# A hybrid Hyena / RG-LRU / latent-attention kernel: the attention's output projection begun inside attention, two layer norms in halves, two steps of the mixer in another order

## The chip, the cores and the metric

The kernel runs on one core of a Trainium2 chip. The number that counts is the device time of one execution in microseconds (us); lower is better. The engines are PE (TensorE, matrix products), DVE (VectorE), ACT (ScalarE), POOL (GpSimd) and SP (SyncE, whose queue issues most DMAs). PEld is PE's loading of the stationary operand, shown apart from the products that stream through it.

## The reference

Two layers work on 512 latent tokens and 256 context tokens of width 1024. A layer is half a SwiGLU feed-forward net, a token mixer, and another half net; each sub-layer is modulated and ends in a layer norm:

```python
x_lat = half_ffn(x_lat, ...)                                  # ends in a layer norm
h_lat = modulate(x_lat, m_lat[3], m_lat[4])
y_lat, y_ctx = even_mixer(...) if l % 2 == 0 else odd_mixer(...)
x_lat = layernorm(ALPHA * x_lat + m_lat[5] * y_lat, ln_g[l, 1], ln_b[l, 1])
x_lat = half_ffn(x_lat, ...)                                  # last layer: latent tokens alone

def layernorm(x, g, b):
    mu = jnp.mean(x, -1); var = jnp.mean((x - mu) ** 2, -1)
    return (x - mu) * lax.rsqrt(var + LN_EPS) * g + b

# odd_mixer: 16 heads of latent attention, 512 queries, 768 keys
o_l = blocked_attention(qn_l, qr_l, k_nope, k_rope, v)        # softmax over keys
out_lat = o_l.reshape(B, L, MLA_HEADS * MLA_V) @ w_out        # 1024 x 1024

# even_mixer: y = x0 * (longconv(v * x1) + bias * ...), beside a gated linear recurrence
Y = rfft(u, n=2 * L) * rfft(k, n=2 * L); y = irfft(Y)[:L]
```

Everything is float32.

## The kernel before, in words

Activations lie in SBUF with the channels on the 128 partitions, in 8 chunks (m or k = 0 to 7), and the tokens along the free axis: 512 latent, then 256 context. A float32 product is made of three: the weight and the activation are each split into a high part (rounded to fp32r) and the rest, and PE adds high x high, high x low and low x high in PSUM (lines 2768 to 2770). Weights come by DMA in pieces of 512 KB (128 x 1024) into two buffers, RAW[0] and RAW[1], by turns. ACT makes the high part of a piece (WHI, line 990), DVE the low part (WLO, line 1619); a piece's buffer is loaded again when its low part is done. There are three pairs of such weight buffers: A, B and W, each for two pieces ("a unit").

All five engines run programs written out by hand, each with its own order, tied by semaphores. An engine that waits holds everything behind it in its program. So the place of an instruction in the code sets the order.

**Even mixer (layer 0).** `even_in` makes its input in ten units; in the last (u == 9) `turned_product` (line 3155) turns the convolution's input by 24 transposes in six groups of four, three PSUM banks in turn; group 3 waits until ACT has taken group 0 (`ut_ok`). Then six forward transforms (`forward(n)`, n = 0 to 5: two for the context, four for the latent tokens) each end in `spectrum(n)` on DVE (line 2397), which multiplies by the filter's spectrum; `recur(7)` (line 2357) is the last of eight steps of the recurrence, 5 instructions on DVE. SP loads the table of a transform (`slab_load`) and the filter's spectrum (`spectra_load`); for n = 4 and 5 both wait for `spectrum(n-2)`. Then come the inverse transforms (lines 3252 and 3261) and the output projection `ev_out`.

**Odd mixer (layer 1).** Attention runs in 64 steps g = 8 i + s: i is the pair of heads, s = 0 to 7 a head's block of 128 queries. In step g PE makes the scores of g (lines 2768 to 2770), turns the probabilities of g - 2 by six transposes (line 3381), and adds half of the values' product of an earlier step (line 3396). DVE takes the row's maximum (line 2620), the low part of the turned probabilities (PTL, line 2598), and scales the probabilities (PR, line 2628). ACT makes the exponential (line 1473) and the high part (PTH, line 1481). POOL makes low parts of queries and keys, and of the heads' outputs (OLO, line 900). A pair of heads gives one chunk of the projection's input, OHI[k] and OLO[k]; the first seven are there before step 63, the eighth only after attention's last product. The projection's eight chunks m, 24 products of 512 columns each, begin behind that (`odd_out`); their units use the weight buffers A, B, A, B. DVE adds each chunk to X (line 2470).

**Layer norm.** PE sums over partitions with a matrix of ones (line 2780), ACT takes the mean MU, DVE centers the 8 chunks (line 1736), ACT squares (line 1222), PE sums the squares (line 2792), ACT takes the root (line 1227), DVE the reciprocal (line 1742), and DVE multiplies the chunks (line 1749). For the next net ACT makes the modulated input H and its high part (lines 979 and 982), DVE its low part HLO (line 1719), and PE starts on chunk k when its HLO is there (lines 2817 to 2819). While both latent and context tokens are alive, these are two parts, one worked on while the other's products run. In the last layer the context is dropped behind the odd mixer, so `ln4` (behind attention) and `final` (at the end) have one part of 512 tokens.

**The end.** After `final`, DVE applies gain and bias (line 2654), PE turns X back (line 3452), ACT copies (line 1557), SP stores four tiles of 512 KB.

## Time and profile before

| | us |
|---|---|
| median of 3 runs | 3003.37 (2999.09 to 3003.84) |
| the profiled execution | 3004.83 |
| its span, first to last instruction | 3003.0 |
| PE busy, in the span | 2886.5 |

PE is the busy engine almost throughout. The page's end times of products are modelled and a product's shown duration overlaps the next, so the pace of PE is read from the starts of products, or from the regular distance of the DVE instructions that take their results. In the timeline a row is one instruction or several alike ("x6"), with the start, the length, and in brackets how long the engine had been idle and what ended that. The places that the change touches are about 885 to 945 us (the mixer's transforms), 2495 to 2625 us (attention's end to the first products of the last net, `ffn3`) and 2950 to 3003 us (the end).

### The profile page before, as it was taken

What the parts mean: (1) busy time and instruction counts of PE and PEld (TensorE: products, weight loads), DVE (VectorE), ACT (ScalarE), POOL (GpSimd) and SP (SyncE); (2) the same over time, 40 slices, a digit from 0 to 9 for tenths busy, and PEclk for the clock granted to TensorE, in tenths of its full rate; (3) what the DMA queues carried; (4) which work ended last, traced back from release to release, by engine and by line L of the source; (5) the groups of instructions that cost most, each with busy time, mean ns of one, the idle gap of its engine ahead of it and who ended that gap; (6) DMA issues with size and microseconds to landing.
All of it is one profiled execution on the core that took longest, in us unless ns stands there. A gap on an engine that the chain in (4) does not pass through costs nothing.

```text
span 3003.0 us, 43415 instructions
## 1 busy us (share of the span) xinstructions
PE 2886.5 (96%) x15883; PEld 2467.9 (82%) x15883; DVE 2035.9 (68%) x3216; ACT 1033.5 (34%) x1586; POOL 283.7 (9%) x393
## 2 busy tenths in 40 slices
PE   5999999999999999999999999999999998899997
PEld 2588989987884878898988899999878997688885
DVE  3377777777668477676776887777776886545444
ACT  0422233325650232232223433332255664422121
POOL 1001000001100100101001000000105561000000
PEclk7899999999999999999999999999999998999998
DMA  7334442221203233444431122222310101233330
GB/s 274 128 118 152 132 142 77 69 71 44 60 28 129 79 118 112 157 132 155 131 96 57 43 64 77 70 63 63 93 40 24 26 19 50 70 105 98 98 98 28
DMA packets 301116, 269.59 MB, mean 90 GB/s; under 512 B 31111, under 2 KB 257263, under 8 KB 300880
## 3 DMA queue, kind: packets, MB, share of 16 engines
q1 hardware_dynamic: 278384, 188.95, 21.0%
q0 software_dynamic: 21760, 76.03, 7.2%
q10 hardware_dynamic: 864, 3.15, 0.3%
q8 instruction: 70, 1.15, 0.2%
q14 instruction: 38, 0.31, 0.0%
HBM read 262.85 MB, written 5.24 MB: 89 GB/s over the span
## 4 chain that ended last, share of the span: by engine, by line
PE 89%; DVE 6%; ACT 2%; DMA 2%; issue 1%; POOL 1%; SPq 0%; ACTq 0%; DVEq 0%; POOLq 0%
PE PSALL L2768 15%; PE PSALL L2770 15%; PE PSALL L2769 15%; PE PSALL L3011 8%; PE PSALL L3012 8%; PE PSALL L3013 8%; PE PSALL L2817 2%; PE PSALL L2689 2%; PE PSALL L2818 2%; PE PSALL L2819 2%; PE PSALL L2792 2%; PE PSALL L3396 1%; PE PSALL L3381 1%; PE PSALL L2731 1%; PE PSALL L3261 1%
## 5 line engine op out<-in xcount | busy, mean ns | idle before, releaser
L1927 DVE SCALAR_TENSOR_TENSOR X<-PSALL,GATE,X 128x512 f32<-128x512 f32 x480 | 279.6, 612 | 102.0 <-PE PSALL L2770 101.4
L3011 PE MATMUL PSALL<-HHI,WSH 128*128 128x384 f32 x816 | 274.8, 337 | 5.6 <-DVE HLO L2125 5.6
L3012 PE MATMUL PSALL<-HLO,WSH 128*128 128x384 f32 x816 | 274.3, 336 | 0.0
L3013 PE MATMUL PSALL<-HHI,WSL 128*128 128x384 f32 x816 | 274.2, 336 | 0.0
L2768 PE MATMUL PSALL<-GHIA,WHIW 128*128 128x512 f32 (+1 forms) x616 | 217.5, 353 | 13.0 <-DVE X L1927 9.9
L2769 PE MATMUL PSALL<-GLOA,WHIW 128*128 128x512 f32 (+1 forms) x616 | 213.7, 347 | 0.0
L2770 PE MATMUL PSALL<-GHIA,WLOW 128*128 128x512 f32 (+1 forms) x616 | 213.1, 346 | 0.0
L2770 PE MATMUL PSALL<-GHIB,WLOW 128*128 128x512 f32 (+1 forms) x616 | 212.8, 346 | 0.0
L2768 PE MATMUL PSALL<-GHIB,WHIW 128*128 128x512 f32 (+1 forms) x616 | 212.8, 345 | 0.0
L2769 PE MATMUL PSALL<-GLOB,WHIW 128*128 128x512 f32 (+1 forms) x616 | 212.7, 345 | 0.0
L3011 PE MATMUL PSALL<-TH,WSH 128*128 128x384 f32 x612 | 208.6, 341 | 0.0
L3012 PE MATMUL PSALL<-TL,WSH 128*128 128x384 f32 x612 | 207.6, 339 | 0.0
L3013 PE MATMUL PSALL<-TH,WSL 128*128 128x384 f32 x612 | 207.5, 339 | 0.0
L1099 ACT ACTIVATE WSH<-RAW 128x512 fp32r<-128x512 f32 x204 | 129.1, 633 | 224.5 <-DVE RAW L2004 151.5
L2768 PE MATMUL PSALL<-HHI,WHIA 128*128 128x512 f32 (+1 forms) x464 | 168.7, 364 | 0.0
L2770 PE MATMUL PSALL<-HHI,WLOA 128*128 128x512 f32 (+1 forms) x464 | 165.3, 356 | 0.0
L2769 PE MATMUL PSALL<-HLO,WHIA 128*128 128x512 f32 (+1 forms) x464 | 165.3, 356 | 0.0
L3011 PEld LDWEIGHTS PSALL<-HHI,WSH 128*128 128x128 f32 x816 | 154.3, 189 | 6.4 <-issue 6.4
L2768 PE MATMUL PSALL<-HHI,WHIB 128*128 128x512 f32 (+1 forms) x432 | 157.9, 366 | 1.3 <-DVE MOD L1609 1.3
L781 POOL DMA_DIRECT2D ADA<-in_ada_w_dram x144 | 76.8, 533 | 847.2 <-PE PSALL L2689 756.9
L2769 PE MATMUL PSALL<-HLO,WHIB 128*128 128x512 f32 (+1 forms) x432 | 155.0, 359 | 0.0
L990 ACT ACTIVATE WHIW<-RAW 128x1024 fp32r<-128x1024 f32 x92 | 96.0, 1055 | 171.4 <-PE PSALL L2770 95.6
(383 smaller groups left out, 7097.3 us busy)
## 6 DMA issues: line engine op xcount, KB each, us to landing
RAW<-in_ffn_w_in_dram SPq DMA_DIRECT2D x176, 512.0 KB, 4.1
ADA<-in_ada_w_dram POOLq DMA_DIRECT2D x144, 512.0 KB, 5.7
RAW<-in_ffn_w_out_dram SPq DMA_DIRECT2D x88, 512.0 KB, 3.9
RAW<-in_ev_w_in_dram SPq DMA_DIRECT2D x20, 512.0 KB, 3.9
WRAW<-in_mla_w_q_up_dram SPq DMA_DIRECT2D x16, 288.0 KB, 3.0
RAW<-in_ev_w_out_dram SPq DMA_DIRECT2D x8, 512.0 KB, 4.6
RAW<-in_mla_w_in_dram SPq DMA_DIRECT2D x8, 512.0 KB, 4.4
RAW<-in_mla_w_out_dram SPq DMA_DIRECT2D x8, 512.0 KB, 4.5
```

Source lines behind the costliest of these rows:

```text
L781: pool.dma_start(ADA[slot][:, :], src).then_inc(ada_in[slot], 16)
L990: act.activation(WHI[slot][:, 1024 * half:1024 * half + 1024], RAW[raw_slot(q)][:, :], ACT.Copy).then_inc(hi_done, 1)
L1099: return act.activation(WSH[:, place, :], raw[:, 512 * cols:512 * cols + 512], ACT.Copy)
L1927: dve.scalar_tensor_tensor(X[:, m, lo:lo + n], down_bank(m, s, 2), GATE[:, j, m, s:s + 1], X[:, m, lo:lo + n], ALU.mult, ALU.add).then_inc ...
L2689: x = te.matmul(PS[3][32 * j:32 * j + 32, 0:D // 4], SC[:, k, :], ADA[slot][:, j * D // 4:(j + 1) * D // 4], start=(k == 0), stop=(k == KC ...
L2768: te.matmul(out, w_hi, x_hi(k), start=(k == 0), stop=False)
L2769: te.matmul(out, w_hi, x_lo(k), start=False, stop=False)
L2770: x = te.matmul(out, w_lo, x_hi(k), start=False, stop=(k == ks - 1))
L2792: x = te.matmul(stat_bank(name, s), ONES[:, :], SQ[:, m, lo:lo + n], start=(m == 0), stop=(m == KC - 1))
L3011: te.matmul(out, w_hi, hi[block](k), start=(k == 0), stop=False)
L3012: te.matmul(out, w_hi, low[block](k), start=False, stop=False)
L3013: x = te.matmul(out, w_lo, hi[block](k), start=False, stop=(k == 3))
```

## The change

**1. Projection inside attention.** `mla_out` uses the weight buffers A, W, B, W. Its chunks 0 to 3 take the seven finished head pairs inside attention's last steps and behind its last turns; the eighth head pair (k = 7) comes after. ACT splits the weights of units 0 and 1 in steps s = 2 and s = 6 of the last pair; POOL instead of DVE makes their low parts (`out_low`). **2. Halves.** Chunks 4 to 7 are made for tokens 0 to 255 and for 256 to 511 apart, and so are `ln4`, `ffn3`'s first pair of units and its last products, and `final`. PE sums the first half's tokens, and its squares, between products of the second. **3. The end.** ACT adds the bias, DVE multiplies by gain and reciprocal root in one instruction, and eight tiles of 256 KB are stored. **4. Mixer.** `turned_product` is cut in two, with 24 products between; the forward tables 0 and 1 share RAW[0] and table 2 lies in RAW[1]; `recur(7)` stands behind `spectrum(3)`; the loads of the inverse tables are reordered, and the second piece of `ev_w_out` is loaded after the context's inverse.

```diff
-    stage("mla_out", q=8, A=4, B=4, evac=8)
-    ln_plan("ln4", 1)
+    stage("mla_out", q=8, A=2, B=4, W=6, evac=12)
+    ln_plan("ln4", 2)
     ffn_plan("ffn3", 1)
-    stage("final", ln=1)
+    stage("final", ln=2)
+    MLA_OUT = [("A", 0), ("W", 0), ("B", 0), ("W", 2)]
...
# SP, even mixer
         for n in range(2):
             slab_load(n)
+        sp.wait_ge(slab_in[0], 16)
+        slab_load(2)
...
+        sp.wait_ge(df_pe, 2)
+        proj_load(A["ev_w_out"][0], 0, plan["ev_out"].q)
+        sp.wait_ge(r_y, RY0 + 2 * (HC - 1))
+        sp.wait_ge(r_scan, 2 * (2 * HC - 1))
+        inverse_load(0)
+        sp.wait_ge(df_pe, 3)
         sp.dma_start(ISLAB[0][:, :].rearrange("p (f n) -> p f n", f=CB_),
                      A["inv_c"].rearrange("f p s t -> p f (s t)")).then_inc(inv_in[0], 16)
         for n in range(4, NF):
             sp.wait_ge(df_y, 4 * (n - 1))
             slab_load(n)
             spectra_load(n)
+        sp.wait_ge(r_y, RY0 + 2 * HC)
+        for b in range(1, LB):
+            inverse_load(b)
+        sp.wait_ge(inv_pe, HC)
+        proj_load(A["ev_w_out"][0], 1, plan["ev_out"].q + 1)
...
# POOL, attention
+            if not more:
+                pool.wait_ge(q_lo, MH)
+                out_low(0)
             if i:
                 heads_low(i - 1)
...
+        out_low(1)
         heads_low(PAIRS - 1)
...
# ACT, attention, layer norm
-                    elif s == 5:
+                    elif s == 2:
                         act.wait_ge(q_pe, MH)
-                        for half in range(2):
-                            split_hi("A", half, b.q + half, 0, b.A)
+                        out_split(0)
+                    elif s == 6:
+                        out_split(1)
...
+            if name == "final":
+                mean(0)
+                for m in range(KC):
+                    square(0, m)
+                mean(1)
+                for m in range(KC):
+                    if m == KC // 2:
+                        root(0)
+                    square(1, m)
+                root(1)
+                return
...
# DVE, even mixer
-            spectrum(0)
-            spectrum(1)
+            for n in range(4):
+                spectrum(n)
             recur(2 * HC - 1)
-            for n in range(2, NF):
+            for n in range(4, NF):
                 spectrum(n)
...
# DVE, output projection of attention
+            chunk(0)
+            chunk(1)
+            dve.wait_ge(lo_done, b.q + 4)
+            weights(2)
+            chunk(2)
+            chunk(3)
+            weights(3)
+            chunk(4, 0)
+            chunk(5, 0)
+            next_unit("ffn3", "A")
+            chunk(6, 0)
+            chunk(7, 0)
+            chunk(4, 1)
+            for m in range(5):
+                center("ln4", 2, 0, m)
+            chunk(5, 1)
+            for m in range(5, KC):
+                center("ln4", 2, 0, m)
+            chunk(6, 1)
             next_unit("ffn3", "B")
+            context("ln4", {0: lambda: chunk(7, 1)})
...
# PE, last net
                 if S == 1:
-                    for m in range(KC):
-                        te.wait_ge(evac, e0 + m - 3)
-                        chunk(0, m, down_bank(m, 0, S))
-                    sums(then, 1, 0, lambda m: e0 + m + 1)
+                    for a in range(2):
+                        for m in range(KC):
+                            te.wait_ge(evac, e0 + KC * a + m - 3)
+                            chunk(0, m, down_bank(m, 0, S)[:, 0:CTX], CTX * a)
+                            if a == 1 and m == 1:
+                                sums(then, 1, 0, lambda m: e0 + m + 1)
+                    sums(then, 1, 1, lambda m: e0 + KC + m + 1)
...
# PE, even mixer
                         if u == 9 and s == 0 and half == 1:
                             gates(u - 2, 1)
-                            turned_product()
+                            turned_product(0, 3)
+                        if u == 9 and s == 1 and half == 0:
+                            turned_product(3, TB)
...
# PE, output projection of attention
+            for m in range(4):
+                chunk(m, None, (KC - 1, KC))
+            te.wait_ge(t_pe, 8 * PAIRS)
+            te.wait_ge(pt_lo, 8 * PAIRS)
+            chunk(4, 0)
+            chunk(5, 0)
+            chunk(6, 0)
+            te.wait_ge(evac, p.evac + 2)
+            chunk(7, 0)
+            te.wait_ge(evac, p.evac + 3)
+            te.wait_ge(o_add, 2 * MH)
+            chunk(4, 1, between=lambda: sums("ln4", 2, 0, evicted(0)))
+            te.wait_ge(evac, p.evac + 4)
+            chunk(5, 1)
+            te.wait_ge(evac, p.evac + 6)
+            chunk(6, 1, between=lambda: variance("ln4", 2, 0))
+            chunk(7, 1)
+            sums("ln4", 2, 1, evicted(1))
...
# PE, attention
+                    if not more and s >= 5:
+                        if s == 5:
+                            te.wait_ge(q_rot, MH)
+                        chunk(0, None, (2 * s - 10, 2 * s - 8))
             turn(8 * PAIRS - 2)
+            te.wait_ge(s_exp, 8 * PAIRS - 1)
+            chunk(0, None, (6, 7))
+            chunk(1, None, (0, 3))
             turn(8 * PAIRS - 1)
-            for e in (4 * PAIRS - 2, 4 * PAIRS - 1):
-                for n in range(2):
-                    outputs(e, n)
+            chunk(1, None, (3, 7))
+            e = 4 * PAIRS - 2
+            for n in range(2):
+                outputs(e, n)
+            chunk(2, None, (0, 7))
+            for n in range(2):
+                outputs(e + 1, n)
+            te.wait_ge(s_exp, 8 * PAIRS)
+            chunk(3, None, (0, 7))
```

What this does to the instructions of an engine, at three places. First PE at attention's end, before; ID x PR are the turns of the probabilities, PTH and PTL the values' products, OHI0 and WHIA the projection's first:

```order
L2770 MATMUL PSALL<-KH1_207,QL1_180 128x256
L3381 MATMUL PSALL<-ID_77,PR1_225 128x128 x6
L3396 MATMUL PSALL<-PTL1_223,VALL_182 128x256 x6
L3381 MATMUL PSALL<-ID_77,PR0_224 128x128 x6
L3381 MATMUL PSALL<-ID_77,PR1_225 128x128 x6
L3396 MATMUL PSALL<-PTH0_220,VALL_182 128x256 x6
L3396 MATMUL PSALL<-PTL0_222,VALL_182 128x256 x6
L3396 MATMUL PSALL<-PTH1_221,VALL_182 128x256 x6
L3396 MATMUL PSALL<-PTL1_223,VALL_182 128x256 x6
L2768 MATMUL PSALL<-OHI0_183,WHIA_55 128x512
```

The same place after, from the last scores to the last but one turn and on:

```order
L2896 MATMUL PSALL<-KH1_206,QL1_179 128x256
L3545 MATMUL PSALL<-ID_77,PR1_224 128x128 x6
L3560 MATMUL PSALL<-PTL1_222,VALL_181 128x256 x6
L3356 MATMUL PSALL<-OHI4_186,WHIA_55 128x512
L3357 MATMUL PSALL<-OLO4_194,WHIA_55 128x512
L3358 MATMUL PSALL<-OHI4_186,WLOA_57 128x512
L3356 MATMUL PSALL<-OHI5_187,WHIA_55 128x512
L3357 MATMUL PSALL<-OLO5_195,WHIA_55 128x512
L3358 MATMUL PSALL<-OHI5_187,WLOA_57 128x512
L3545 MATMUL PSALL<-ID_77,PR0_223 128x128 x6
L3356 MATMUL PSALL<-OHI6_188,WHIA_55 128x512
L3357 MATMUL PSALL<-OLO6_196,WHIA_55 128x512
```

Products of the projection now stand between the last steps: six each in steps 5, 6 and 7, then twelve behind each of the last two turns, and 21 behind each of the last two values' products.

Second, DVE behind attention, before; WLOA and WLOB are low parts of weights (the last WLOA and WLOB are `ffn3`'s):

```order
L2470 SCALAR_TENSOR_TENSOR X<-PSALL,GATE,X 128x512 x2
L1619 TENSOR_TENSOR WLOA<-RAW_54,WHIA 128x1024
L1619 TENSOR_TENSOR WLOA<-RAW_53,WHIA 128x1024
L2470 SCALAR_TENSOR_TENSOR X<-PSALL,GATE,X 128x512 x2
L1736 TENSOR_TENSOR X<-X,MU 128x512 x8
L1619 TENSOR_TENSOR WLOB<-RAW_54,WHIB 128x1024
L1619 TENSOR_TENSOR WLOB<-RAW_53,WHIB 128x1024
L1742 RECIPROCAL RSTD<-RSTD 128x512
L1749 TENSOR_TENSOR X<-X,RSTD 128x512 x2
```

And after:

```order
L2613 SCALAR_TENSOR_TENSOR X<-PSALL,GATE,X 128x256 x2
L1711 TENSOR_TENSOR WLOA<-RAW_54,WHIA 128x1024
L1711 TENSOR_TENSOR WLOA<-RAW_53,WHIA 128x1024
L2613 SCALAR_TENSOR_TENSOR X<-PSALL,GATE,X 128x256 x3
L1828 TENSOR_TENSOR X<-X,MU 128x256 x5
L2613 SCALAR_TENSOR_TENSOR X<-PSALL,GATE,X 128x256
L1828 TENSOR_TENSOR X<-X,MU 128x256 x3
L2613 SCALAR_TENSOR_TENSOR X<-PSALL,GATE,X 128x256
L1711 TENSOR_TENSOR WLOB<-RAW_54,WHIB 128x1024
L1711 TENSOR_TENSOR WLOB<-RAW_53,WHIB 128x1024
L1834 RECIPROCAL RSTD<-RSTD 128x256
L1841 TENSOR_TENSOR X<-X,RSTD 128x256 x3
```

`ffn3`'s low part of A stands ahead of the additions of chunks 6 and 7 (first half), and that of B ahead of the reciprocal and of the last addition, chunk 7 of the second half, which follows the three multiplications.

Third, DVE in the mixer, before; YC and YL are spectra of context and latent tokens, RT and GATED belong to `recur(7)`:

```order
L2414 TENSOR_TENSOR YC_150<-YC_150,TMP_162 128x512
L2363 TENSOR_TENSOR RT_134<-RT_134,RT_142 128x770
L2369 SCALAR_TENSOR_TENSOR RT_134<-RT_140,RT_134 128x256
L2371 SCALAR_TENSOR_TENSOR RT_134<-RT_140,RT_134 128x512
L2375 TENSOR_TENSOR RT_134<-RT_134,RT_133 128x770
L2377 TENSOR_TENSOR GATED<-GATED,RT_134 128x770
L2407 TENSOR_TENSOR YL_146<-PSALL,KFS_158 128x512
```

And after, around the end of `spectrum(3)`:

```order
L2521 TENSOR_TENSOR YL_151<-YL_151,TMP_161 128x512
L2470 TENSOR_TENSOR RT_134<-RT_134,RT_142 128x770
L2476 SCALAR_TENSOR_TENSOR RT_134<-RT_140,RT_134 128x256
L2478 SCALAR_TENSOR_TENSOR RT_134<-RT_140,RT_134 128x512
L2482 TENSOR_TENSOR RT_134<-RT_134,RT_133 128x770
L2484 TENSOR_TENSOR GATED<-GATED,RT_134 128x770
L2514 TENSOR_TENSOR YL_146<-PSALL,KFS_157 128x512
```

The five instructions of the recurrence's last step moved behind two more spectra.

## Rows read from the trace of the kernel before

**Rows 1.** The page, part 1: busy us (share of the span) xinstructions.
```profile
PE 2886.5 (96%) x15883; PEld 2467.9 (82%) x15883; DVE 2035.9 (68%) x3216; ACT 1033.5 (34%) x1586; POOL 283.7 (9%) x393
```

**Rows 2.** Windows view: stretch, busy us (instructions) per engine, granted clock, DMA share, GB/s.
```profile
2478.00:2534.00 56.00, 44.99 (x269) 39.88 (x269) 39.80 (x71) 29.07 (x50) 11.11 (x8) 0.86 0.13 38
```

**Rows 3.** Timeline, PE, even mixer: start us, us, engine, line, work, idle before.
```profile
889.72 2.30 PE L3165 MATMUL PSALL<-ID,U 128*128 128x128 f32 x12 [3.18 <-ACT UTL L1318]
...
906.20 13.97 PE L3239 MATMUL PSALL<-UTL,SLAB 128*128 128x512 f32 x32 [0.70 <-DVE YC L2414]
...
922.58 14.00 PE L3239 MATMUL PSALL<-UTL,SLAB 128*128 128x512 f32 x32 [2.41 <-DMA SLAB<-in_fwd_l_dram]
```

**Rows 4.** Timeline, DVE, even mixer.
```profile
909.98 0.96 DVE L2363 TENSOR_TENSOR RT<-RT,RT 128x770 f32<-128x770 f32 x1
...
915.01 0.69 DVE L2407 TENSOR_TENSOR YL<-PSALL,KFS 128x512 f32<-128x512 f32 x1
```

**Rows 5.** Timeline, SP's queue, even mixer.
```profile
918.92 0.34 SPq L675 DMA_DIRECT2D SLAB<-in_fwd_l_dram  x1
```

**Rows 6.** Timeline, PE, attention's end.
```profile
2521.03 0.85 PE L3381 MATMUL PSALL<-ID,PR 128*128 128x128 f32 x6 [2.17 <-DVE PTL L2598]
...
2534.30 0.63 PE L2768 MATMUL PSALL<-OHI,WHIA 128*128 128x512 f32 x1
```

**Rows 7.** Timeline, DVE, attention's end.
```profile
2505.92 0.96 DVE L2620 TENSOR_REDUCE STAT<-PSALL 128x1 f32<-128x768 f32 x1
...
2508.86 0.95 DVE L2620 TENSOR_REDUCE STAT<-PSALL 128x1 f32<-128x768 f32 x1
...
2513.69 0.94 DVE L2620 TENSOR_REDUCE STAT<-PSALL 128x1 f32<-128x768 f32 x1
...
2516.61 2.35 DVE L1619 TENSOR_TENSOR WLOA<-RAW,WHIA 128x1024 fp32r<-128x1024 f32 x2
```

**Rows 8.** Timeline, ACT, attention's end.
```profile
2510.92 1.99 ACT L990 ACTIVATE WHIA<-RAW 128x1024 fp32r<-128x1024 f32 x2
```

**Rows 9.** Timeline, POOL, output projection.
```profile
2546.88 1.29 POOL L797 TENSOR_TENSOR RSTD<-X 128x512 f32<-128x512 f32 x1 [9.46 <-DVE X L2470]
```

**Rows 10.** Timeline, DVE, both output projections.
```profile
1015.84 0.88 DVE L2470 SCALAR_TENSOR_TENSOR X<-PSALL,GATE,X 128x256 f32<-128x256 f32 x2 [4.88 <-PE PSALL L2770]
...
2547.20 3.19 DVE L1619 TENSOR_TENSOR WLOA<-RAW,WHIA 128x1024 fp32r<-128x1024 f32 x2 [0.40 <-ACT WHIA L990]
...
2567.81 0.75 DVE L2470 SCALAR_TENSOR_TENSOR X<-PSALL,GATE,X 128x512 f32<-128x512 f32 x1 [4.69 <-PE PSALL L2770]
...
2568.96 2.36 DVE L1619 TENSOR_TENSOR WLOA<-RAW,WHIA 128x1024 fp32r<-128x1024 f32 x2 [0.40 <-ACT WHIA L990]
```

**Rows 11.** The page, part 6: DMA, KB each, median us to landing.
```profile
RAW<-in_mla_w_out_dram SPq DMA_DIRECT2D x8, 512.0 KB, 4.5
```

**Rows 12.** Timeline, PE, layer norm behind attention.
```profile
2585.11 7.11 PE L2792 MATMUL PSALL<-SQ,ONES 128*128 128x512 f32 x16 [2.17 <-ACT SQ L1222]
...
2599.47 0.79 PE L2817 MATMUL PSALL<-HHI,WHIA 128*128 128x512 f32 x1 [7.26 <-DVE HLO L1719]
```

**Rows 13.** Timeline, DVE, a 256-wide layer norm, and the residual before ffn3.
```profile
1031.62 1.75 DVE L1742 RECIPROCAL RSTD<-RSTD 128x256 f32<-128x256 f32 x1 [0.45 <-ACT RSTD L1227]
...
2609.23 3.74 DVE L1728 TENSOR_SCALAR X<-X,AG,AB 128x512 f32<-128x512 f32 x8
```

**Rows 14.** Timeline, ACT, a 256-wide layer norm.
```profile
1033.86 0.60 ACT L979 ACTIVATE H<-X,CB,CG 128x256 f32<-128x256 f32 x1 [2.28 <-DVE X L1749]
```

**Rows 15.** Timeline, PE, the program's end.
```profile
2971.56 8.80 PE L2792 MATMUL PSALL<-SQ,ONES 128*128 128x512 f32 x16 [2.17 <-ACT SQ L1222]
...
2993.11 5.32 PE L3452 MATMUL PSALL<-ID,X 128*128 128x128 f32 x32 [12.75 <-DVE X L2654]
```

**Rows 16.** Timeline, ACT, the program's end.
```profile
2996.72 2.56 ACT L1557 ACTIVATE OUT<-PSALL 128x512 f32<-128x512 f32 x5 [0.15 <-PE PSALL L3452]
```

**Rows 17.** The page, part 5: weight loads (PEld), count, busy us, mean ns.
```profile
L3011 PEld LDWEIGHTS PSALL<-HHI,WSH 128*128 128x128 f32 x816 | 154.3, 189 | 6.4 <-issue 6.4
```

282 lines of the change are left out of this document (172 added, 110 removed).

## The prediction

> **What bounds the kernel now.** I read the page's part 1 first [rows 1]: PE is busy for 96% of the span, DVE for 68%, ACT 34%, POOL 9%. So a change wins where it lets PE work in time that it now waits, or where it removes waits; it can't win by relieving DVE alone. PE's busy time itself hardly changes here: the 192 products of 512 columns of the projection are still made, partly as twice as many of 256.
>
> Then I read PE's timeline at the three places that the order shows as changed. In the mixer PE waits 3.18 us before the fourth group of transposes, 0.70 before transform f2 and 2.41 before f4 [rows 3]. At attention's end the window of 56 us has 44.99 us of PE work at a mean granted clock of 0.86 [rows 2]; the turns wait 2.17 us for PTL of DVE, and the projection's first product starts at 2534.30 [rows 6]. The mean of 0.86 says that over a quarter of the window ran at 1.2 GHz rather than 2.4. Behind the projection come the layer norm's serial steps: the 16 products with ones wait 2.17, then `ffn3`'s first product waits 7.26 [rows 12], and at the end the same again, with 12.75 us of idling before the last transposes [rows 15]. These are the places to cover.
>
> The paces that I use: a float32 chunk of 48 products of 256 columns in 0.88 + 4.88 = 5.76 us between two additions for two chunks of 24, thus 0.12 us a product; 24 products of 512 in 0.75 + 4.69 = 5.44, thus 0.227 [rows 10]. A half-width product costs 0.0065 more than half of a wide one.
>
> **A. Mixer.** The cut of `turned_product` puts 24 products of 256 into its 3.18 us wait: 24 x 0.12 = 2.9 gained. `recur(7)` runs on DVE from 909.98 to 915.01 ahead of `spectrum(2)` [rows 4]. f2 starts at 906.20 and its first half of 32 products ends about 913.1, so without `recur(7)` the spectrum starts near 913.2, 1.8 earlier. The table of f4 is issued 3.9 behind that start, at 918.92 [rows 5], and lands just ahead of f4's start at 922.58; its wait of 2.41 [rows 3] shrinks by 1.8. The 0.70 stays. The moved loads (inverse tables, second piece of `ev_w_out`, each one or a few DMAs on SP) fall under the context's inverse and have an estimated 7 us or more to spare; `recur(7)`, now behind `spectrum(3)`, lies under f4 and f5 and is needed first by the output projection. Sum A: -4.7. Ends: -2.5 (the transposes now wait for something else) and -5.5 (the 0.70 too).
>
> **B. Attention's end to the second unit of ffn3.** *Projection inside attention.* Before, the fourth chunk's result is taken at 2567.81 - 2 x 5.44 = 2556.9 [rows 10]. After, PE does in the waits of the last steps 18 products, behind the last turns 24, between and behind the last values' products 42: 84 products, which is chunks 0 to 3 with seven head pairs; then 12 for the eighth. What sets a step's length is DVE and ACT, not PE: a plain step is 2508.86 - 2505.92 = 2.94 from reduction to reduction, and the one in which ACT splits a unit's weights 2513.69 - 2508.86 = 4.83 [rows 7]. The 18 products, 4.1 us in three steps, fit into PE's waits. Of ACT's pair of 1.99 [rows 8] I take 1.0 as what it costs a step, since part of the 4.83 is an added DVE operation; there are two such steps after and one before: +1.0. POOL makes four low parts of 128x1024: a 128x512 operation with two inputs takes it 1.29 [rows 9], so 2.6 each, 10.3 in all, against some 25 us from step s = 2 to the first use of unit 1.
>
> POOL's cost to others: DVE's pairs of low parts beside POOL's work take 3.19 instead of 2.36 [rows 10]. So DVE loses 0.83 in 2.36 when POOL works; for four low parts of POOL, with DVE's PR and PTL beside them, I take +1.8 (0 to 3.6, the last if DVE waited 0.9 for each). The Trainium skill, "SBUF — State Buffer", section "SBUF: two separate sides", says that the pair of ports shared by VectorE and GpSimd is locked for a whole instruction, and that the loser blocks fully. By that a DVE instruction with two SBUF inputs could wait up to a whole 2.6 us low part, four times 10 us. The rows show that beside a POOL instruction of 1.29 two DVE instructions lengthen by 0.83 together, which would fit a lock of part of one.
>
> The 2.35 us of DVE's low part at 2516.61 [rows 7] go. So the turn of step 62 starts at 2521.03 [rows 6] + 1.0 + 1.8 - 2.35 = 2521.5, with 18 products done. From there PE never waits: two turns (0.6 each at 2.4 GHz), four groups of the values' products (0.7 each) and 66 + 12 products at 0.227, 21.7 us in all, end at 2543.2. Gain at chunk 3: 2556.9 - 2543.2 = 13.7; I take 13.3. Some 5 us of it come because the stretch at 1.2 GHz is filled.
>
> *Chunks 4 to 7 in halves.* 192 x 0.12 = 23.0 against 96 x 0.227 = 21.8. Waits that I see ahead of them: 0.8 for a low part behind additions 0 and 1, 0.6 for a DMA of 4.5 us [rows 11] whose buffer comes free late, 2.5 because the additions of chunks 6 and 7 stand behind `next_unit("ffn3", "A")` on DVE and the sums wait for them. The first half's sums and squares go between products: 8 with ones at 0.27 and 8 at 0.43 (16 in 7.11 wait-bound for 512 columns [rows 12]), 5.6 us. End of the last chunk: 2543.2 + 23.0 + 3.9 + 5.6 = 2575.7, before 2578.7 (2567.81 + 2 x 5.44).
>
> *The norm.* Before, from the last addition to `ffn3`'s first product: 2599.47 - 2578.7 = 20.8. After, the first half's mean and root are already there. On DVE the last addition stands behind WLOB's 2.36, the half reciprocal 1.75 [rows 13] and the first norms, about 1.1; first product near 2579.7, gain 19.8. But then it is a series again: eight chunks of H and HHI on ACT at 0.60 + 0.34 = 0.94 each [rows 14] are 7.5 us for 24 products of 0.12 (before: 24 of 0.227), the squares of the second half 3.4, 5.8 for the other weights' 48 products, 96 products of 256 for the second half 11.5, and 1.7 of waiting for DVE, which has 16 residual operations where it had 8 in 3.74 [rows 13] as well as HLO: 29.9 us. Before: 96 x 0.227 + 2.1 at the lower clock = 23.9. Second unit: 2579.7 + 29.9 = 2609.6 against 2599.47 + 23.9 = 2623.4. Sum B: -13.8, of which I take -13.1, since three of these waits were sized as if nothing came together. Ends: -8 (POOL's blocking at its full 3.6, ACT's splits late by 3 more) and -19 (the four waits gone and the clock at 2.4 throughout).
>
> **C. The end.** Before: the last 48 products of 512 take 10.9, then the sums, the squares until 2971.56 + 8.80 = 2980.4, the reciprocal, norms, gain and bias, transposes from 2993.11 [rows 15], last OUT at 2996.72 + 2.56 = 2999.3 [rows 16], span's end 3003.0: 3.7 behind. After: the first half is centred and squared while the second half's products run, so the sums of the second half end near 2969.7; the squares of the first half (8 x 0.43 = 3.4) and of the second follow to 2973.1 and 2976.6. Reciprocal 0 is done at 2975.7 (1.75 [rows 13], start behind root 0), eight multiplications of 256 at 0.44 take until 2979.2, reciprocal 1 until 2981.0, eight more until 2984.5; bias on ACT, transposes and copies follow in order, the last copy ends near 2989.6, and the store's 3.7 give 2993.3. Sum C: 2993.3 - 3003.0 = -9.7. The reciprocal's first half is covered and one of three DVE passes (norm, gain, bias) gone. Ends: -7.5 (ACT, which now has bias and copies, is last: 16 biases of about 0.35 partly ahead of the copies) and -11.
>
> **Sum.** -4.7 - 13.1 - 9.7 = -27.5. The profiled execution took 3004.83, 1.83 outside its span of 3003.0: 3004.83 - 27.5 = 2977.3. It stands 1.46 above the median of 3003.37, so on the median's footing 2975.9; I say 2976.
>
> **Rivals.**
> *R1, slow: the products of 256 are bound by their weight loads.* Each product loads 128x128 weights; where such loads are listed they take 189 ns on average [rows 17], more than 0.12. The change makes 192 products of 256 in chunks 4 to 7, 192 in the first pair of units and 96 at the end, 480 for which it had 240. If each took 0.19, 480 x 0.07 = 33.6 us would be lost against my sum: 2975.9 + 33.6 = 3009.5. It decides above a spacing of 0.12 + 27.5 / 480 = 0.177. For it: PEld is 82% busy [rows 1]. Against it: 48 products of 256 at 0.12 each behind one another, with a load each [rows 10]. Chance 0.04. The Trainium skill, "TensorE: Matmul & The Clock Gate", section "The mechanism", says that a weight load overlaps products in flight only when its row group differs; these loads use all 128 rows, so by that rule none would overlap. The trace disagrees as far as it goes: loads of 189 ns could not lie inside a spacing of 120 otherwise.
> *R2, the clock falls in attention's end as before.* If DVE's chain still leaves PE short in steps 5 to 7, the granted clock falls to 1.2 GHz and the 84 products take 0.43 instead of 0.227 for about 10 us: +5, 2981. For it: 0.86 in the window [rows 2]. Against it: each wait now has six products in it. 0.15.
> *R3, the softmax chain is held by weight splits.* ACT's pairs of 1.99 [rows 8] and POOL's 2.6 stand in the steps' period; if each of four blocks delays the chain by 1.7 more, +7: 2983. For it: the step of 4.83 [rows 7] has ACT's pair in it. Against it: ACT is only 52% busy there (29.07 of 56 [rows 2]). 0.16.
> *R4, the halves don't do what they say.* Both norms' halves run one behind the other on DVE and ACT, and the second half's chain is as late as the whole was: C gives 3, B's norm 3 less: 2975.9 + 6.7 + 3 = 2985.6. For it: ACT works each chunk at 0.94, wide or not nearly the half. 0.08.
> The forecast, 2976: 0.57.
>
> **How the numbers follow.** The forecast's own range, from the sum of the ends taken as independent, is 2970 to 2982. With R2 and R3 inside and R4 partly, 2966 to 2987 holds 8 in 10. A measurement of this kernel can tell about 0.2% (6 us) from no change: faster needs under 2997.4. All but R1 and a combination of R3 with R4 and the small ends of A to C are below: faster 0.91, same 0.04, slower 0.05.
>
> **What would show it.** In the profile after: PE's wait inside `turned_product` under 0.5, f4's wait under 1; between the last scores and the fourth addition no PE wait above 1 us, granted clock near 1 in a window of the same 56 us; the spacing of 256-wide products 0.12 in chunks 4 to 7; the fourth addition 13 us earlier against its distance from the last scores; `ffn3`'s first product about 20 earlier, its second unit about 13 to 14; at the end 3.7 us behind the last OUT, and the span between the last net's down products and the end about 40.7 instead of 50.4. Wrong it would be if DVE's reductions in steps 2 to 7 stood further apart than before, which would be R3, or if PE waited for additions 6 and 7 for more than 4 us.

## The result, and the profile after

The changed kernel takes 2977.0 us (median of 4 runs, 2976.0 to 2978.4) where the one before takes 3002.0 beside it (median of 4, 2999.1 to 3003.8). The ratio is 0.9919 with a 95% interval of 0.9903 to 0.9935: 25 us faster, and within the forecast's range. The forecast was 2976, which meant 27.4 us off the 3003.4 that it started from; the runs beside the changed kernel put the kernel before at 3002.0. The span fell from 3003.0 to 2974.6, by 28.4; why this is 3.4 more than the medians say comes out below.

Part 1 of the page of the profile and the windows view of attention's end and of the stretch behind it (columns as in [rows 1, 2]):

```profile
PE 2880.1 (97%) x16175; PEld 2483.8 (84%) x16175; DVE 2037.0 (68%) x3266; ACT 1044.4 (35%) x1638; POOL 296.9 (10%) x403
```

```profile
2474.00:2534.00 60.00, 56.49 (x330) 49.44 (x329) 37.89 (x64) 29.11 (x48) 18.63 (x11) 0.97 0.18 53
```

PE's busy time changed by 6 us in 2886; what went is waiting. In attention's last 60 us PE is busy for 56.5, where it was 45.0 of 56 [rows 2], and the granted clock is 0.97, not 0.86.

The timeline of PE in the mixer, after:

```profile
886.47 1.54 PE L3291 MATMUL PSALL<-ID,U 128*128 128x128 f32 x12 [0.40 <-ACT UTL L1384]
...
898.38 7.11 PE L3403 MATMUL PSALL<-UTL,RAW 128*128 128x512 f32 x16 [0.63 <-DVE YC L2521]
...
913.41 7.13 PE L3403 MATMUL PSALL<-UTL,SLAB 128*128 128x512 f32 x16 [1.05 <-DMA SLAB<-in_fwd_l_dram]
```

The wait of 3.18 [rows 3] is 0.40, f4's of 2.41 is 1.05, and the 0.70 stayed at 0.63. The twelve transposes last 1.54 and not 2.30: in the trace before, the granted clock falls behind the wait (a mean of 0.59 from 889.7 to 893.7), and here it does not (1.00 from 886.4 to 890.4).

PE at attention's end and behind it, after (each line the first of a stretch, or one with a wait):

```profile
2500.30 0.63 PE L2894 MATMUL PSALL<-KH,QH 128*128 128x512 f32 x1
...
2504.14 0.39 PE L3356 MATMUL PSALL<-OHI,WHIA 128*128 128x512 f32 x1
...
2513.16 0.85 PE L3545 MATMUL PSALL<-ID,PR 128*128 128x128 f32 x6
...
2535.97 0.36 PE L3356 MATMUL PSALL<-OHI,WHIB 128*128 128x256 f32 x1 [0.71 <-DVE WLOB L1711]
2536.16 0.28 PE L3357 MATMUL PSALL<-OLO,WHIB 128*128 128x256 f32 x1
2536.28 0.28 PE L3358 MATMUL PSALL<-OHI,WLOB 128*128 128x256 f32 x1
...
2552.06 1.13 PE L2905 MATMUL PSALL<-X,ONES 128*128 128x256 f32 x4 [0.75 <-DVE X L2613]
...
2569.86 0.70 PE L2905 MATMUL PSALL<-X,ONES 128*128 128x256 f32 x2 [1.43 <-DVE X L2613]
2570.38 0.39 PE L2940 MATMUL PSALL<-HHI,WHIA 128*128 128x256 f32 x1
...
2600.85 0.50 PE L2894 MATMUL PSALL<-HHI,WHIA 128*128 128x512 f32 x1 [1.49 <-DVE WLOA L1711]
...
2620.19 0.50 PE L2894 MATMUL PSALL<-GHIA,WHIW 128*128 128x512 f32 x1 [2.62 <-DVE X L1913]
```

The projection starts inside step 61 (s = 5), the last turns have no wait ahead of them (2.17 in [rows 6]), products of 256 columns follow each other by 0.12, and `ffn3`'s first product waits for nothing (7.26 in [rows 12]). Of the new waits, two lie in the net, at 2600.85 and at 2620.19; the others, of 0.61 to 1.43, lie ahead of it.

The end after, PE's last transposes and ACT's last copy:

```profile
2966.08 1.97 PE L3627 MATMUL PSALL<-ID,X 128*128 128x128 f32 x8 [2.50 <-ACT X L1631]
2969.52 1.97 PE L3627 MATMUL PSALL<-ID,X 128*128 128x128 f32 x8 [1.48 <-ACT X L1631]
```

```profile
2971.53 0.60 ACT L1636 ACTIVATE OUT<-PSALL 128x512 f32<-128x512 f32 x1 [0.26 <-PE PSALL L3627]
```

The wait of 12.75 before the transposes [rows 15] is gone; four smaller ones, of 0.26 to 2.50, stand in and ahead of them.

To see where the time went I cut every trace at the same places, by the starts of instructions: the first transposes of `turned_product`; the first product of the context's inverse; DVE's reduction of step 56, the first of the last pair; the fifth chunk's first product; `ffn3`'s first product; the first product of its second unit; its last down products; the end. Lengths in us, rounded so that they add up to the spans:

| stage | before | after | forecast of the difference | measured |
|---|---|---|---|---|
| start to the mixer's transposes | 885.1 | 881.7 | 0 | -3.4 |
| mixer | 51.3 | 45.5 | -4.7 | -5.8 |
| from there to the last pair | 1554.9 | 1555.0 | 0 | +0.1 |
| attention's end and chunks 0 to 3 | 65.4 | 53.8 | -13.7 (taken: -13.3) | -11.6 |
| chunks 4 to 7 and layer norm | 42.8 | 34.4 | -6.1 | -8.4 |
| `ffn3`, first units | 23.9 | 30.4 | +6.0 | +6.5 |
| `ffn3`, second unit to the last down products | 329.2 | 332.6 | 0 | +3.4 |
| the end | 50.4 | 41.2 | -9.7 | -9.2 |

### The profile page after: what moved, and what is told of

The parts are those of the page before. It is cut to its first block, busy times and chain, and to the rows that moved or that the text cites. A ratio compares the mean times of both kernels' runs of the same rounds, so it can differ in the third digit from the quotient of the medians.

```text
span 2974.6 us, 44155 instructions
## 1 busy us (share of the span) xinstructions
PE 2880.1 (97%) x16175; PEld 2483.8 (84%) x16175; DVE 2037.0 (68%) x3266; ACT 1044.4 (35%) x1638; POOL 296.9 (10%) x403
## 4 chain that ended last, share of the span: by engine, by line
PE 88%; DVE 6%; DMA 2%; ACT 2%; issue 1%; POOL 1%; SPq 0%; ACTq 0%; POOLq 0%; DVEq 0%
PE PSALL L2894 14%; PE PSALL L2896 14%; PE PSALL L2895 14%; PE PSALL L3137 8%; PE PSALL L3138 8%; PE PSALL L3139 8%; PE PSALL L2815 2%; PE PSALL L2940 2%; PE PSALL L2941 2%; PE PSALL L2942 2%; PE PSALL L2916 2%; PE PSALL L3560 1%; PE PSALL L3545 1%; PE PSALL L2857 1%; DMA RAW<-in_ffn_w_in_dram 1%
## 5 line engine op out<-in xcount | busy, mean ns | idle before, releaser
L837 POOL TENSOR_TENSOR RSTD<-X 128x256 f32<-128x256 f32 (+1 forms) x12 | 15.2, 1269 | 1426.1 <-DVE X L2258 877.2
```

## The experiments

Times are medians of several runs beside runs of the kernel before on the same chip, whose medians lay between 3000.5 and 3003.6; runs of one kernel scatter by 2 to 6 us either way. So small differences are read from the stages of the traces, and the medians are the check. The ratio of each kernel to the kernel before beside it is a second check; for the changed kernel it is 0.9919, a gain of 24.

**The parts one by one.** e1 is the kernel before with the mixer's edits alone:

```diff
-                            turned_product()
+                            turned_product(0, 3)
+                        if u == 9 and s == 1 and half == 0:
+                            turned_product(3, TB)
...
-            spectrum(0)
-            spectrum(1)
+            for n in range(4):
+                spectrum(n)
             recur(2 * HC - 1)
```

> The kernel before with the mixer's part alone (turned_product cut in two, forward tables moved, recur(7) behind spectrum(3), reordered loads). Theory: the two traces of before and after lie 3.4 us apart already ahead of the mixer, where the programs are the same, which is scatter between executions, and 5.7 us more apart behind it. So this kernel is 5 to 6 us faster than before (the forecast's term was 4.7), about 2996.5, and its trace shows the offset to before grow between 880 and 945 us, by 4.4 at the transposes and by 1.4 at f4's wait. Rival: the early 3.4 us belong to the change too (the moved loads), then 9 us faster.

Measured: 2995.7 beside 3000.9, 5.2 faster (by the ratio of 0.9986, 0.9977 to 0.9995, it is 4.2, or 1.5 to 6.9). PE's timeline in the mixer of e1:

```profile
887.89 1.54 PE L3177 MATMUL PSALL<-ID,U 128*128 128x128 f32 x12 [0.40 <-ACT UTL L1330]
...
914.51 14.00 PE L3253 MATMUL PSALL<-UTL,SLAB 128*128 128x512 f32 x32 [0.72 <-DMA SLAB<-in_fwd_l_dram]
```

The mixer takes 45.2 (before 51.3), every stage behind it what it took before to 0.3. Its transposes start at 883.1, 1.9 earlier than in the trace of before, and up to there the two programs are the same. In all traces this start lies between 881.3 and 885.8, in no relation to the edits. So the 3.4 us are scatter, and the rival of 9 us fell.

e2 is the changed kernel with its end as before (one part of 512, gain and bias on DVE, four stores):

```diff
-    HALVED = ('ln4', 'final')
+    HALVED = ('ln4',)
-    stage("final", ln=2)
+    stage("final", ln=1)
```

> The changed kernel with its end as before: last products of 512 columns, the layer norm `final` in one part, gain and bias on DVE, four stores. Theory: the end is worth its own 9.2 us (the forecast's term was 9.7), so this is 9 to 10 us slower than the changed kernel, about 2986. Rival: the halves at the end give back part of it through the wait of 2.4 us that the first half's additions show; then only 7.

Measured: 2984.4, 7.4 slower than the changed kernel; in its trace the end takes 50.6, against 41.2. The median fits the rival, the trace the theory, and the scatter of the runs covers the difference of 2. The ratio (0.9952, against 0.9919) makes it 9.9 slower and so sides with the trace. In this trace the stages ahead of the end are those of the changed kernel, but for the start (1.9 later) and 2.3 us in the unchanged middle (1552.6).

e3 is the changed kernel with the early products put back behind attention:

```diff
-                        chunk(0, None, (2 * s - 10, 2 * s - 8))
...
+            for e in (4 * PAIRS - 2, 4 * PAIRS - 1):
+                for n in range(2):
+                    outputs(e, n)
+            for m in range(4):
+                chunk(m, None, (0, 7))
```

> The changed kernel, but PE makes chunks 0 to 3 only behind attention's last values' product; weights, low parts and all other orders as changed. Theory: the 84 products filled time in which PE waited or ran at 1.2 GHz, so they cost 84 x 0.227 = 19 us when put behind, less what the last steps get shorter without them (about 7): 11 to 13 us slower than the changed kernel, about 2989. The granted clock falls again behind the last scores. Rival: the last steps are bound by DVE and ACT and don't get shorter at all: 19 us slower, 2996.

Measured: 2989.1, 12.1 slower (13.8 by the ratios). Attention's end takes 67.1 and not 53.8. The windows view of e3, and two lines of PE in it:

```profile
2474.00:2534.00 60.00, 47.95 (x273) 42.01 (x273) 38.53 (x65) 29.86 (x51) 19.44 (x12) 0.86 0.18 53
```

```profile
2513.63 0.85 PE L3545 MATMUL PSALL<-ID,PR 128*128 128x128 f32 x6 [2.19 <-DVE PTL L2732]
...
2527.45 0.63 PE L3356 MATMUL PSALL<-OHI,WHIA 128*128 128x512 f32 x1
```

The waits before the turns and the clock of 0.86 are back, with weights and low parts as in the change. The 84 products take 84 x 0.227 = 19 us behind attention; inside it they cost 13.3 less, thus 6. Three parts of the change are 4.2 to 6.1, 12.1 to 13.8 and 7.4 to 9.9 us; their sum of 23.7 to 29.8 leaves little or nothing of the 25 measured for the halves behind attention.

**The halves behind attention.** e10 undoes them alone:

```diff
-    HALVED = ('ln4', 'final')
+    HALVED = ('final',)
...
-            chunk(4, 0)
-            chunk(5, 0)
+            chunk(4)
+            chunk(5)
             next_unit("ffn3", "A")
```

> The changed kernel with chunks 4 to 7, the layer norm behind attention and the last net's first units in one part of 512 tokens, as before the change; the projection's early products, the mixer and the end stay changed. By the stages of the traces, from the fifth chunk to the last down products the changed kernel takes 34.4 + 30.4 + 11.1 + 321.5 = 397.4 us and the kernel before 42.8 + 23.9 + 10.9 + 318.3 = 395.9. Theory: the halves here gain 8.4 us ahead of the net's first product, give 6.5 back in its first units (192 products of 256 paced by ACT's chunks, squares between) and 3.2 in the wait at the first down products; undoing them costs nothing: between 3 us faster and 0 (about 2975.5). Rival: the 3.2 are not theirs but come from the earlier weights' order; then 2 us slower, about 2979.

Measured: 2975.9 (changed kernel 2977.0, and 2978.0 in e11; by the ratio of 0.9905 it is 4 faster). Its norm stage takes 44.4, the first units 24.1, the rest of the net 329.2, in sum 397.7; the changed kernel's three stages are 397.4, and 399.6 in e11. PE of e10 at the net's first product:

```profile
2579.95 0.80 PE L2934 MATMUL PSALL<-HHI,WHIA 128*128 128x512 f32 x1 [7.17 <-DVE HLO L1811]
```

The wait of 7.2 us is back and costs no more than the halves' later waits. So halving this norm gained what it gave back, and the 3.4 us of later waits are its own: with 512 columns they are gone (329.2, as before). The rival fell. The norm stage of e10 is 1.7 longer than that of the kernel before (42.7): it has a wait of 0.81 for WLOB, and behind the same wait of 2.17 for the squares the clock is 0.72 over 6 us, where it was 1.00.

**What made the new waits.** On DVE the 16 residual operations stand ahead of the weights. e6 moves them behind the two low parts of WLOA:

```diff
-        residual("ln4", 1, 5)
-        ffn("ffn3", 1, 5, 0, 0, "final", None)
+        ffn("ffn3", 1, 5, 0, 0, "final", None, late=lambda: residual("ln4", 1, 5))
...
                 split_lo(slot, half, p.q + q, 0)
+                if late is not None and e == 1:
+                    late()
```

> The changed kernel, with DVE's 16 residual operations of the last net (5.26 us) moved behind GMA, GHI, GLO and the two low parts of WLOA. Theory: they are what makes the net's weight chain (low part, buffer free, DMA, high part) late: PE waits 1.49 for WLOA at the second unit and 2.62 at the first down products, and the offset to before falls from 22.4 to 19.1 us there. With this edit WLOA is made 2.2 us earlier, the wait of 1.49 goes and that of 2.62 shrinks below 2: the time falls by 2 to 3, about 2974.5. Rival: the chain is bound by the DMAs' own pace of 3 us a piece and by PE's late release of the A weights; then 0 to -1, and the 2.62 grows by what the 1.49 shrinks.

Measured: 2977.7, no gain. The first units take 28.8 and not 30.4, as the theory had it, but the rest of the net takes 336.2 and not 332.6 (or 334.2, in e11). PE of e6, and its windows:

```profile
2619.49 0.79 PE L2897 MATMUL PSALL<-GHIA,WHIW 128*128 128x512 f32 x1 [3.84 <-DVE X L1913]
...
2625.20 0.54 PE L2898 MATMUL PSALL<-GLOA,WHIW 128*128 128x512 f32 x1
```

```profile
2619.50:2640.00 20.50, 20.50 (x78) 16.73 (x79) 9.79 (x13) 3.60 (x5) 0.00 (x0) 0.85 0.33 103
```

The wait at the first down products grew from 2.62 to 3.84, and behind it PE ran at 1.2 GHz until 2625 (a product each 0.43, 13 of them). The theory failed and the rival's numbers held, with the clock on top.

The clock is not a matter of these 1.2 us of waiting alone. In the first trace of the changed kernel it did not fall behind the 2.62; in e11, the same kernel with a wait of 2.50, it did, 1.5 us after PE had gone on:

```profile
2621.17 0.50 PE L2894 MATMUL PSALL<-GHIA,WHIW 128*128 128x512 f32 x1 [2.50 <-DVE X L1913]
...
2622.70 0.63 PE L2894 MATMUL PSALL<-GHIA,WHIW 128*128 128x512 f32 x1
...
2626.09 0.39 PE L2896 MATMUL PSALL<-GHIA,WLOW 128*128 128x512 f32 x1
```

Over the 11 us that begin 17 us into the second unit the granted clock is 1.00 in the changed kernel's first trace and in e2, whose rest of the net takes 332.6 and 332.4; it is 0.84 in e3, e4, e5 and e11 (333.7 to 334.2), and 0.69 in e6 and e7 (336.2 and 335.9). The waits of the first six are 2.27 to 2.76 and don't sort them; those of e6 and e7 are 3.84 and 3.51.

What makes PE wait there? DVE of the changed kernel:

```profile
2616.05 0.68 DVE L1888 TENSOR_TENSOR GMA<-GMA,PSALL 128x512 f32<-128x512 f32 x1
2618.24 1.23 DVE L1711 TENSOR_TENSOR WLOA<-RAW,WHIA 128x1024 fp32r<-128x1024 f32 x1 [1.51 <-ACT WHIA L1044]
2619.39 1.41 DVE L1913 SCALAR_TENSOR_TENSOR X<-PSALL,GATE,X 128x512 f32<-128x512 f32 x2
```

and ACT, for the same piece:

```profile
2617.16 1.06 ACT L1044 ACTIVATE WHIA<-RAW 128x1024 fp32r<-128x1024 f32 x1 [1.80 <-DMA RAW<-in_ffn_w_in_dram]
```

PE waits for an addition that needs nothing but PE's own result. It stands on DVE behind a low part, whose high part waits for a DMA. e8 lets the additions go first:

```diff
-                    if e in (0, 2 * S) and todo and not last:
+                    if e in ((0, 2 * S) if S == 2 else (2, 4)) and todo and not last:
```

> The changed kernel; in the last net's loop DVE makes the two low parts of WLOA behind the second and the fourth addition of the down products, not ahead of the first and the third. In the changed kernel's trace PE waits 2.62 us for the first addition of the first down products (X of DVE at 2619.39), which stands on DVE behind a low part at 2618.24 whose high part waited for a DMA; the late residual (e6) only made this wait 3.84. Theory: with the additions first, that wait goes, since the banks' results were there at 2613 to 2617; the low parts are still early enough for the next unit: 2 to 3 us faster than the changed kernel, about 2974.5, and the length from the first down products to the last ones falls from 321.5 to below 319.5 (before: 318.3). Rival: the weight chain itself is late, and PE then waits as long at the next unit for WLOA: no change, 2977.

Measured: 2973.2 (ratio 0.9897, 0.9879 to 0.9914), 3.8 below the changed kernel. DVE and PE of e8:

```profile
2617.45 1.41 DVE L1913 SCALAR_TENSOR_TENSOR X<-PSALL,GATE,X 128x512 f32<-128x512 f32 x2
2618.76 1.22 DVE L1711 TENSOR_TENSOR WLOA<-RAW,WHIA 128x1024 fp32r<-128x1024 f32 x1
```

```profile
2612.69 0.49 PE L2894 MATMUL PSALL<-GHIA,WHIW 128*128 128x512 f32 x1 [0.41 <-DVE GLOB L1900]
```

Of the wait of that place 0.41 is left, and from the second unit to the last down products e8 takes 330.2, where six traces with the old order and the residual in its place take 332.4 to 334.2. So the weights were early enough; their place was the fault, and the order is worth 2.2 to 4.0 us, the upper part of it where the clock would have fallen. This trace starts the mixer 4.1 us later than the changed kernel's and takes 2.4 less in the unchanged middle and 1.0 less at the end, so its span and median say less of the edit than the stage does. With the additions first, the three stages behind attention's end are 394.0 in e8 and 395.0 in e12, against 397.7 with 512 columns (e10) and 395.9 before. e10 and the kernel before have no wait in the rest of the net, so there the order has nothing to remove; with it the halved norm is worth 1 to 4 us.

**POOL and DVE.** The changed kernel in attention's end, DVE and then POOL:

```profile
2488.68 0.62 DVE L2762 TENSOR_SCALAR PR<-PR,STAT 128x768 f32<-128x768 f32 x1
...
2495.18 0.96 DVE L2732 TENSOR_TENSOR PTL<-PSALL,PTH 128x768 fp32r<-128x768 f32 x1 [0.72 <-ACT PTH L1547]
...
2496.26 2.50 DVE L2762 TENSOR_SCALAR PR<-PR,STAT 128x768 f32<-128x768 f32 x1
...
2513.14 2.15 DVE L2762 TENSOR_SCALAR PR<-PR,STAT 128x768 f32<-128x768 f32 x1
```

```profile
2493.64 4.69 POOL L958 TENSOR_TENSOR WLOA<-RAW,WHIA 128x1024 fp32r<-128x1024 f32 x2 [1.20 <-ACT WHIA L1044]
...
2510.12 4.75 POOL L958 TENSOR_TENSOR WLOW<-RAW,WHIW 128x1024 fp32r<-128x1024 f32 x2 [6.73 <-ACT WHIW L1044]
```

PR takes 0.62, but 2.50 and 2.15 where it starts inside POOL's pair; both end 0.4 behind the pair's end (2498.33 and 2514.87). The excess of each, 1.88 and 1.53, is what was left of POOL's instruction when PR started (2.07 and 1.73), less 0.2. PTL, which reads PSUM, takes 0.96 in the midst of the same pair, as elsewhere. e4 makes each low part by two instructions of 128x512:

```diff
-                pool.tensor_tensor(WLO[slot][:, cols], RAW[raw_slot(q + half)][:, :], WHI[slot][:, cols].bitcast(F32),
-                                   ALU.subtract).then_inc(lo_done, 1)
+                for piece in range(2):
+                    at = 1024 * half + 512 * piece
+                    x = pool.tensor_tensor(WLO[slot][:, at:at + 512], ...)
+                x.then_inc(lo_done, 1)
```

> The changed kernel, with each of POOL's four low parts of weights made by two instructions of 128x512 in place of one of 128x1024. In the changed kernel's trace two of DVE's PR instructions (128x768, 0.62 us elsewhere) take 2.50 and 2.15, and each ends just behind the end of a POOL low part of 2.35. Theory (an instruction of POOL holds DVE's PR out until that instruction is over): with pieces of 1.2 the two PR take at most 1.8 each, so the sum of their excess falls from 3.4 to 1 to 2 and attention's end comes 1 to 2 us earlier; the time falls by 1 to 2, about 2975.5. Rival (the two share bandwidth, or it is the pair of low parts as a whole that holds PR out): the excess stays 3.4, time unchanged at 2977.

Measured: 2976.3 by the median; in the trace attention's end takes 51.5 and not 53.8, more than the 1 to 2 expected. DVE of e4:

```profile
2500.77 1.54 DVE L2764 TENSOR_SCALAR PR<-PR,STAT 128x768 f32<-128x768 f32 x1
...
2515.30 1.20 DVE L2764 TENSOR_SCALAR PR<-PR,STAT 128x768 f32<-128x768 f32 x1
```

The two excesses are 0.92 + 0.58 = 1.5 and not 1.88 + 1.53 = 3.4, and PE's wait behind the first is 1.27 and not 2.22. The score products of 512 columns that took 0.63 each behind the 2.22 take 0.40 here, at 2.4 GHz. The medians, whose runs lie between 2969.7 and 2981.0, don't resolve it; e7, e9 and e12, which have the pieces too, show 51.5 as well. By the Trainium skill, "SBUF — State Buffer", section "SBUF: two separate sides", a GpSimd instruction locks the shared port pair for its whole length and a VectorE one that needs it is blocked. The trace agrees: both PR end just behind POOL's current instruction (by 0.4), and POOL's instructions of 1.3 hold for less than those of 2.35.

e5 takes the low parts from POOL and puts them on DVE, two behind the PR of step 3 and two behind that of step 7 of the last pair:

```diff
-                out_low(0)
...
-        out_low(1)
...
+                    if s in (3, 7) and not more:
+                        u = s // 4
+                        dve.wait_ge(q_lo, MH)
+                        for half in range(2):
+                            split_lo(MLA_OUT[u][0], half, b.q + 2 * u + half, 0)
```

> The changed kernel, with the low parts of units 0 and 1 on DVE (behind the PR of steps 3 and 7 of the last pair) and not on POOL. Theory: DVE works 4 x 1.2 = 4.7 us more on the softmax chain and is spared the 3.4 that POOL costs it; net +1.3, or 0 to +2, as a part of the work in step 7 lies beside waits: about 2978. Rival: POOL's low parts cost nothing but the two long PR, which lie beside waits anyway: then +4 to +5, about 2981.

Measured: 2978.6; attention's end takes 54.5, 0.7 more than on POOL, and each PR 0.62. The theory's +1.3 is nearer than the rival's +4 to +5. So moving 4.7 us of work from DVE to POOL was worth 0.7 by the traces, because POOL cost DVE 3.4 of it; in pieces it is worth 3.0.

**Together.** e7 has the pieces and the late residual, e9 the additions first as well, e12 all but the late residual, and e11 is the changed kernel again.

> The pieces on POOL and the late residual together: the sum of the two, 3 to 5 us below the changed kernel by the two theories, about 2973; no difference by the two rivals.

Measured: 2975.5. Attention's end is 51.5 and the first units 28.8, but the rest of the net takes 335.9: the late residual is lost again, the pieces' 2.3 stay.

> Additions first, the late residual and POOL's pieces together. Theory: the late residual's 1.6 to 1.8 us at the second unit are now kept, since no longer wait follows in which the clock falls; with the pieces' 2.3 (from their trace) and the additions' 2.6 this is 5 to 7 us faster than the changed kernel, about 2971. Rival: as for the additions alone, the chain is late whatever the order; then 2 to 3, about 2974.5.

> The changed kernel once more, on the same chip as the next one and with more runs. Its stage lengths should repeat those of its first trace to 0.3 us where no DMA decides (mixer 45.5, attention's end 53.8, norm 34.4, first units 30.4), and its median lie at 2977, 25 below the kernel before. If the scatter ahead of the mixer (882 to 886 us in nine traces) is all that separates its first span from its time, the span will differ from 2974.6 by what this stretch does.

> The changed kernel with the additions first and POOL's low parts in pieces, but the residual where it was. Theory: of the three edits the late residual gives 1.6 us (first units 28.8 and not 30.4), so this kernel is 1.6 slower than the one with all three, about 2972. Rival: once the additions stand first, the residual's place makes no difference, since the wait for WLOA's DMA takes its 1.5 anyway: 2970.5.

Measured: e9 2970.6 (ratio 0.9888, 0.9871 to 0.9904), the fastest here, 6.4 below the changed kernel and 5 to 7 were expected. e11 2978.0 and e12 2971.7, on one chip. e11's stages are 45.7, 53.7, 34.9, 30.4, 334.2 and 41.2: all repeat to 0.5 (0.3 was expected, and the norm's stage misses it) but the rest of the net (332.6 in the first trace), in which the clock fell; its start at 882.4 is 0.7 later, its span 2.4. So the start is not all that separates a span from another, as I had put it: the net's 1.6 is the larger part. e12's median lies 1.1 above e9's; in the traces the late residual gives 1.7 in the first units and loses 0.6 behind them, where e9 has a wait of 0.85 for an addition. The difference of the medians is within the scatter. e9's trace also has 1.5 us from its end (39.7, against 41.2), where its code is the changed kernel's.

## Why the prediction was right

The number is right (2976, measured 2977.0), and the gain less exactly so: 27.4 forecast, 25.0 measured. Most sizes held; the errors of the parts were of both signs and add up to 3.1 us too much gain, of which the forecast had itself taken off 0.7 (its parts of B, -13.7, -6.1 and +6.0, are -13.8, and it entered -13.1). That the level is hit to 1.0 is in part luck: the kernel before ran 1.4 faster beside the changed one than in the runs that the forecast started from.

*What bounds it.* Right: PE's busy time stood still and its waits went.

*A, the mixer: -4.7, measured -5.8 (e1: -6.1 in the trace).* The mechanism was right in both halves. The transposes' part was too small: the step counted only the 24 products in a wait, 2.9, and not that PE came out of this wait at 1.2 GHz, which the transposes (2.30 us [rows 3], 1.54 after) and the first products behind them paid; the two traces drift 4.4 apart from the first transposes to the first transform. f4's wait shrank by 1.36 and not by 1.8 (by 1.7 in e1).

*B, projection inside attention: -13.3 taken, measured -11.6.* Right in kind, and e3 shows it. The turn of step 62 was to start 0.5 later against the last pair than before; by the traces, brought to one another by their offset of 9.1 at the pair's start, it starts 1.2 later, where POOL held DVE's PR for 3.4 and not for the 1.8 that I took (the bound was 3.6). From there to chunk 3's end PE needed 22.1, forecast 21.7. A wait of 0.71 for WLOB comes behind. I also misread the row that I held against a hold for the whole instruction: POOL's 1.29 begins at 2546.88 [rows 9] and DVE's pair at 2547.20 [rows 10], so 0.97 of POOL's instruction was left, and the 0.83 that the pair lost is nearly all of it. The rule of the Trainium skill on the ports ("SBUF — State Buffer", section "SBUF: two separate sides") fits that row and was the right one for PR.

*Chunks 4 to 7 and the norm: -6.1 (2579.7 - 2543.2 against 2599.47 - 2556.9), measured -8.4.* Spacing, sums and squares were as forecast; the wait for additions 6 and 7 was 0.75 and not 2.5. `ffn3`'s first product came 20.0 earlier against the same offset (2599.47 - 2570.38 - 9.1), forecast 19.8.

*The net's first units: +6.0, measured +6.5*, with 1.49 of waiting for WLOA where I had 1.7. The second unit came 22.6 - 9.1 = 13.5 earlier, forecast 13.8 by the terms and 13.1 as entered.

*The step that failed* is that the account of B was closed at the second unit, so that what lies behind it was put at nothing. I had asked what waits up to there and not what DVE's weights do to the unit behind. The weight chain leaves the norm 5 to 6 us later against PE than before. The last low part of WLOA begins 0.1 us ahead of the second unit, where it began 5.7 ahead; the first WHIW is made 3.6 us behind the unit's start (2604.47), where it was made 2.1 ahead of it before, as it still is with 512 columns (2.2). The additions stand behind this chain, and the net loses 3.4 us (2.62 of it in one wait), and 5.0 in e11, where the clock fell too. e8 removes all but 1.0, e6 removes nothing, and e10 shows that it is the halves' price: in the changed kernel's order the halved norm is worth nothing or a little less. The -6.1 and the +6.0 had it at -0.1, so what the forecast missed is the 3.4 alone.

*C, the end: -9.7, measured -9.2 by the trace*, 7.4 by e2's median. Right, by two errors that cancel: the last copy ends 38.7 behind the stage's start (2933.4) where the terms had 37.0, and the span ends 2.4 behind that copy, not 3.7.

*The rivals.* R1, products of 256 bound by their weight loads: no, they follow by 0.12 in every chunk. By the Trainium skill, "TensorE: Matmul & The Clock Gate", section "The mechanism", loads overlap products only in other row groups; at 0.12 a product, with loads that mean 192 ns in chunks 4 to 7, the trace disagrees once more. The same section also names a background weight buffer into which a load can go ahead; the trace does not contradict that. R2, the clock: 0.97, no. It did fall for the six score products that start at 2500.30 (three of 512 columns at 0.63, three of 256 at 0.41), behind a wait of 2.22 for DVE, which the first held PR had kept; with POOL's pieces (e4, e7, e9, e12) it does not, and in e5, where the low parts on DVE make that wait 2.61, it does. R3, the softmax chain held by splits: half right, in its place and not in its size. From step 2's reduction to step 7's it is 20.2 us (2490.38 to 2510.56), before 19.4, so 0.8 where I gave it 7. R4, halves that do nothing: false for the end and, in the order that the changed kernel has, true in effect for the norm behind attention, though not by its mechanism: the norm's stage did get 8.4 shorter, and it was given back later.

*The sum.* -5.8 - 11.6 - 8.4 + 6.5 + 3.4 - 9.2 = -25.1, which is also the difference of the medians; that the profiled run's stages agree with it so closely is partly chance, since e11's would give 2 less. The profiled run of before started 3.4 us later into the mixer than the one of after; this makes the spans' 28.4.

## What to carry to other kernels

When an edit brings a consumer forward, follow the weights and buffers behind it for one unit more than the edit touches: a gain that ends in the next wait for a DMA is given back there. On an in-order engine put what the bounding engine waits for ahead of what waits for a DMA; here this one line was worth 2 to 4 us, and with it most of another saving (1.1 of 1.7 us by the traces) was kept. A long instruction on POOL held DVE's SBUF-to-SBUF work for up to 1.9 of its 2.35 us, so move work there in short pieces. Before a difference of 1 to 3 us between two traces is put down to an edit or a wait, compare the granted clock of the stage in both.
